# Quarter numbers of the overflow lists from a copy in SBUF instead of four further loads

## What is computed

```python
logits = (xf @ w_router) + b_router                 # 512 x 32
top_val, top_idx = lax.top_k(logits, 4); gates = softmax(top_val)
for e in range(32):                                 # each over the tokens that chose e
    hu  = x_e @ w_gate_up[e] + b_gate_up[e]          # 1024 -> 2048
    act = a * sigmoid(1.702 * a) * (lin + 1)         # a, lin: clamped halves of hu
    y  += gate * (act @ w_down[e] + b_down[e])       # 1024 -> 1024
```

## Time and profile before

| | us |
|---|---|
| median of three runs | 1307.02 |
| the three runs | 1302.45, 1307.02, 1308.0 |
| the profiled execution | 1307.7 |
| its span, first to last instruction | 1305.9 |
| TensorE matmul busy | 1267.0 (97%) |
| VectorE busy | 577.8 (44%) |
| GpSimd busy | 313.9 (24%) |
| ScalarE busy | 177.3 (14%) |
| moved by DMA | 450.85 MB, 345 GB/s over the span |

### The profile page before, as it was taken

The page is one execution under the profiler, slowest core; times in us unless marked ns, Lnnn a source line. Parts: engine busy times, 40 slices in busy tenths (PEclk is TensorE's granted clock), DMA queues, the critical chain, the costliest instruction groups (busy, mean ns, idle before and its releaser), DMA issues.

```text
span 1305.9 us, 32785 instructions
## 1 busy us (share of the span) xinstructions
PE 1267.0 (97%) x13828; PEld 648.3 (50%) x13828; DVE 577.8 (44%) x977; ACT 177.3 (14%) x254; POOL 313.9 (24%) x315
## 2 busy tenths in 40 slices
PE   6999999999999999999999999999999999999996
PEld 6867777763455444444444443333433333433442
DVE  7676655554444344333333333333333333433435
ACT  5143434310000000000000000000000000000002
POOL 2035522001333332222222222222222222222210
PEclk9999999989999999999999999999999999999998
DMA  9222114579999999999999999999999999999984
GB/s 261 67 65 65 65 65 159 229 302 403 414 415 413 401 375 418 416 421 415 414 412 413 415 417 421 417 418 419 422 419 417 418 417 418 418 418 416 418 361 149
DMA packets 95710, 450.85 MB, mean 345 GB/s; under 512 B 12288, under 2 KB 37360, under 8 KB 46528
## 3 DMA queue, kind: packets, MB, share of 16 engines
q1 hardware_dynamic: 83856, 428.37, 80.5%
q0 software_dynamic: 9760, 19.56, 5.7%
q10 hardware_dynamic: 2064, 2.50, 0.5%
HBM read 440.13 MB, written 18.67 MB: 351 GB/s over the span
## 4 chain that ended last, share of the span: by engine, by line
PE 67%; DMA 27%; DVE 3%; issue 1%; ACT 1%; SPq 1%; DVEq 0%; ACTq 0%
PE gu_bank L1707 32%; DMA raw<-in_w_gate_up_dram 26%; PE bank L1721 15%; PE bank L1481 4%; PE bank L1483 4%; PE bank L1482 4%; PE first_gu_bank L1707 2%; PE bank L1558 1%; PE bank L1572 1%; SPq L417 1%; PE bank L1535 1%; PE bank L1683 1%; PE bank L1724 0%; PE bank L1544 0%; PE bank L1492 0%
## 5 line engine op out<-in xcount | busy, mean ns | idle before, releaser
L1707 PE MATMUL gu_bank<-raw,xT 128*32 128x512 f32 x2976 | 328.5, 593 | 8.5 <-DMA raw<-in_w_gate_up_dram 8.5
L1360 DVE TENSOR_TENSOR gate_in<-gu_bank,b_gu 128x768 f32<-128x768 f32 x31 | 29.7, 958 | 540.0 <-PE gu_bank L1707 540.0
L1707 PEld LDWEIGHTS gu_bank<-raw,xT 128*32 128x32 f32 x2976 | 104.3, 110 | 226.7 <-issue 183.0
L613 POOL DMA_INDIRECT x_got<-xn_rows,gather_list x96 | 114.4, 1192 | 329.1 <-DVE xT L1371 295.7
L1721 PE MATMUL bank<-raw_a,aT 128*32 128x256 f32 x2232 | 166.4, 379 | 0.0
L1707 PE MATMUL gu_bank<-raw_c,xT 128*32 128x512 f32 x1488 | 165.7, 592 | 0.0
L1724 PE MATMUL bank<-raw_a,aT 128*32 128x256 f32 x744 | 165.6, 379 | 0.0
L1721 PEld LDWEIGHTS bank<-raw_a,aT 128*32 128x32 f32 x2232 | 101.2, 110 | 67.7 <-issue 17.4
L902 ACT ACTIVATE sig_in<-gate_in 128x768 f32<-128x768 f32 x32 | 27.0, 845 | 634.0 <-DVE gate_in L1364 634.0
L1707 PEld LDWEIGHTS gu_bank<-raw_c,xT 128*32 128x32 f32 x1488 | 53.2, 110 | 106.4 <-issue 96.5
L623 POOL DMA_INDIRECT sum_rows<-y_out,scatter_list x31 | 46.6, 1504 | 186.9 <-ACT y_out L909 94.8
(11 more groups left out here) (267 smaller groups left out, 1620.1 us busy)
## 6 DMA issues: line engine op xcount, KB each, us to landing
raw<-in_w_gate_up_dram SPq DMA_DIRECT2D x128, 1024.0 KB, 27.7
raw_c<-in_w_gate_up_dram SPq DMA_DIRECT2D x62, 1024.0 KB, 26.0
raw_a<-in_w_down_dram SPq DMA_DIRECT2D x62, 1024.0 KB, 27.6
raw_b<-in_w_gate_up_dram SPq DMA_DIRECT2D x32, 1024.0 KB, 26.1
raw_b<-in_w_down_dram SPq DMA_DIRECT2D x32, 1024.0 KB, 26.9
raw_e<-in_w_gate_up_dram SPq DMA_DIRECT2D x31, 1024.0 KB, 27.3
raw_d<-in_w_down_dram SPq DMA_DIRECT2D x31, 1024.0 KB, 26.8
raw<-in_w_in_dram SPq DMA_DIRECT2D x24, 512.0 KB, 6.3
```

The source lines that it names most:

```text
L613: pool.indirect_dma_start(out=x_got[:, r, :], out_offset=None, in_=xn_quarters, in_offset=bass.IndirectOffsetOnAxis(ap=gather_list[:, r:r ...
L1360: dve.tensor_tensor(gate_in[:, :, :], gu[:, :, 0:QUARTER], gate_b, ALU.add)
L1707: ins = pe.matmul(gu[c * GROUP:(c + 1) * GROUP, r, :], x[:, i, r * GROUP:(r + 1) * GROUP], w[:, c], start=first, stop=last)
```

## The change

The loads into list_q go, and with them list_q, quarter_of and its memsets. After the one load into lists_sb, GpSimd makes the quarter numbers from it with twelve tensor_scalars: for each group r of 32 rows and each quarter c it reads the tokens on partitions 32r to 32r+31 of lists_sb (every second word) and writes 4 x token + c to partitions 32c to 32c+31 of rows_q. Each of the twelve waits for the one before.

```diff
-            list_q = lists_only.enter_context(nc.sbuf_tensor("list_q", [P, GROUPS, PLACES - E, 2], U32))
-        quarter_of = sb("quarter_of", [P, 1])
@@ after the memset of x_got
-            pool.wait_ge(x_got_cleared, 1)
-            for c in range(COLS):
-                pool.memset(quarter_of[c * GROUP:(c + 1) * GROUP, :], float(c)).then_inc(quarters_made, 1)
-                pool.wait_ge(quarters_made, c + 1)
@@ def load_overflow():
                 pool.dma_start(lists_sb[0:TILE, 2 * E:2 * PLACES],
                                lists.rearrange("(s j) c -> s (j c)", s=TILE)[:, 2 * E:2 * PLACES])\
                     .then_inc(lists_held, 16)
-                overflow = lists.rearrange("(r t j) w -> t r j w", r=GROUPS, t=GROUP)[:, :, E:PLACES, :]
-                for c in range(COLS):
-                    pool.dma_start(list_q[c * GROUP:(c + 1) * GROUP, :, :, :], overflow).then_inc(lists_held, 16)
-                pool.wait_ge(lists_held, 16 * (1 + COLS))
-                pool.wait_ge(quarters_made, COLS)
-                pool.tensor_scalar(rows_q[:, :, E:PLACES], list_q[:, :, :, 0], float(COLS), quarter_of[:, :],
-                                   ALU.mult, ALU.add).then_inc(rows_q_made, 1)
-                pool.wait_ge(rows_q_made, GROUPS * COLS + 1)
+                pool.wait_ge(lists_held, 16)
+                tokens = lists_sb[:, 2 * E:2 * PLACES].rearrange("s (j two) -> s j two", two=2)[:, :, 0]
+                for r in range(GROUPS):
+                    for c in range(COLS):
+                        pool.tensor_scalar(rows_q[c * GROUP:(c + 1) * GROUP, r, E:PLACES], tokens[r * GROUP:(r + 1) * GROUP, :],
+                                           float(COLS), float(c), ALU.mult, ALU.add).then_inc(rows_q_made, 1)
+                        pool.wait_ge(rows_q_made, GROUPS * COLS + COLS * r + c + 1)
```

More of the change, by code:

```diff
@@ L276, in build @@
         got_turned, x_turned, x_gained = sem("got_turned"), sem("x_turned"), sem("x_gained")
-        quarters_made, rows_q_made = sem("quarters_made"), sem("rows_q_made")
+        rows_q_made = sem("rows_q_made")
         gu_taken, gate_clamped, lin_clamped = sem("gu_taken"), sem("gate_clamped"), sem("lin_clamped")
```

## The result

| | us |
|---|---|
| changed kernel, median of 4 runs | 1315.85 (1315.36 to 1317.77) |
| kernel before, median of 4 runs beside it | 1306.45 |
| ratio | 1.0088, 95% interval 1.0070 to 1.0106 |
| profiled execution of the changed kernel, its span | 1315.36, 1313.6 |

What follows compares the result with a forecast made beforehand. DMA backlog was taken to bound the late jobs. Profiled 1307.7 - 4.4 (list loads) + 0 (GpSimd) + 0 (addresses) = 1303.3 us; as a median 1307.0 - 4.4 = 1302.6 us, 8-in-10 range 1299.0 to 1308.0.

Steps and rivals of the forecast that it cites:

- The reading of what bounds the kernel: From about 400 us DMA is never out of work and has slightly more to do per job than TensorE gives time for.
- landing time as gauge of backlog: Weight load's time from issue to landing shows DMA backlog; climbs 1.06 us a job, TensorE waits at 28.4 us.
- lost time kept to the end: DMA time spent once, at any time after about 400 us, is still there at the end.
- The lists' term: Removing the four list_q loads, in flight around 450 to 464 us, saves 4.4 us; bounds 1.4 to 5.5.
- The share of 4 in 5: Four of five equal list loads were charged by count with 4/5 of the 5.45 us excess: 4.4 us.
- rival (b): Dent split otherwise: lists_sb makes most, 1305.6 us (chance 0.07), or list_q makes all, 1300.5 to 1301.5 us (0.10).
- the first wait for a weight load: Sign: TensorE's first wait on a load comes three to seven jobs later than 751 us.
- GpSimd's part: Twelve tensor_scalars from about 456.5 us take 5 us (4.8 to 9.6); gather for job 7 has cover, so 0 us.
- Moved, addresses: Without quarter_of all behind it, eight of twelve ring slots included, slides 32 bytes: costs 0 to 0.2%, taken as 0.
- rival (c): Weight loads into eight of twelve slots move more slowly after the 32-byte shift: about 1317 us; chance 0.05.
- a climb of landing time other than 1.06 us a job: Sign that the prediction is wrong: the landing time's climb per job changes from 1.06 us, meaning alignment.

Runs made afterwards that it cites:

- e9: Kernel before with four more list loads of 144 KB, each into 32 partitions of a second tensor: 1308.9 us, ratio 1.0026.
- e1: Changed kernel with 32 unused bytes where quarter_of lay, so later addresses are those of the kernel before: 1301.6 us, ratio 0.9969.
- f4: Changed kernel with the 32 bytes put back, the same kernel as e1, in another group of runs: 1302.72 us, ratio 0.9978.
- e3: Kernel before with quarter_of allocated last of the small tensors, so these slide 32 bytes and the overlay stays: 1305.57 us, ratio 0.9999.
- e10: Kernel before with four more list loads of 144 KB, each into 96 partitions: 1308.58 us, ratio 1.0023.
- f2: Changed kernel with 32 unused bytes ahead of x_got alone: x_got on 256, ring slots 224 past: 1310.48 us, ratio 1.0042.
- f3: Changed kernel with the 32 bytes put back and 224 unused bytes ahead of x_got alone: 1302.56 us, ratio 0.9975.
- e4: Changed kernel with the 32 bytes put back and 128 more ahead of raw01 and of the overlay, all twelve slots on 256: 1297.54 us, ratio 0.9934.
- g4: The same kernel as e4 once more, in another group of runs: 1299.12 us, ratio 0.9948.
- g3: Changed kernel with the 32 bytes put back, plus 128 unused bytes ahead of the overlay: 1309.66 us, ratio 1.0038.
- (g): g3 against g1, 128 and 32 unused bytes ahead of the overlay, on the changed kernel with its 32 bytes put back: 1309.66 and 1314.17 us.
- (e): 128 against 32 unused bytes ahead of the overlay (32 is e5), both on the kernel before: ratios 1.0013 and 1.0055.
- f1: Changed kernel once more, ring slots and x_got both 224 past 256: 1316.25 us, ratio 1.0065.
- g1: Changed kernel with the 32 bytes put back, plus 32 unused bytes ahead of the overlay: 1314.17 us, ratio 1.0069.
- e5: Kernel before with 32 unused bytes ahead of the overlay: ratio 1.0055.
- e8: Kernel before with x_got's, gate_in's, y_out's and b_dn's groups 224 bytes further, ring slots left on 256: ratio 0.9998.

## Why the prediction was wrong, step by step

**The reading of what bounds the kernel held.** DMA behind a TensorE that looks 97% busy, landing time as gauge of backlog, lost time kept to the end: e9 and e1 bear it out in both directions, and the 13 us themselves are such time.

**The lists' term was about right: 4.4 forecast, 4.0 and 2.9 measured with addresses kept** (e1, f4), 3.4 in e9. The share of 4 in 5 is not shown. In e1 the gauge loses 5.9 of its jump of 6.5, which is the whole excess and is what rival (b) had for list_q alone; the first wait for a weight load comes at 1028.69 us in e1 and 965.91 in f4, nine and seven jobs after that of the kernel before, where three to seven were forecast (e3, with the slots and loads of before, has it at 844.66, so this sign is coarse). The time at the end says 3 to 4 us. The Trainium skill's rule on ports ("SBUF — State Buffer", "Door 1: The DMA port swizzle"), by which I had estimated 4.8 us, is neither borne out nor excluded: e9 and e10 have 3.4 and 3.0 us, with intervals that overlap.

**GpSimd's part held.** Twelve instructions 5.25 us (forecast 5), no waiting caused.

**The step that failed is "Moved, addresses ... costs 0 to 0.2%, and I take 0".** It costs 13 us, three times the gain: in each job the weights' queue moves 1.5% less, which the sign I had named for it, a climb of landing time other than 1.06 us a job, showed at once (1.25). I had this as rival (c), at 1317 us where 1315.85 was measured. Its kind was right, its place only in part (x_got's gathers pay too, f2 and f3), and its price agrees by luck: the 2.3% between 418 and 428 GB/s is there with all on 256 as well (f4's twelfths have a mean of 417, because of the dip to 341 in the fifth). I gave it 0.05, because the earlier trace rows showed 427 GB/s while slots of raw, 128 past 256, were filled and 428 while others were. Two things were wrong with that reading. It took for granted that the loss goes with the slot that is being filled. The table of twelfths shows that it goes with the time in the job, and both stretches of the earlier trace rows reach into times where even the changed kernel moves 422 to 429. And it took raw01 for a stand-in: in e4 and g4 the queue shows at most 0.2 MB for raw01 at 128 past, while the overlay at 128 past costs 0.7 MB in five jobs (g3). I should have seen that no row could tell: neither a slot of the overlay nor x_got stood off 256 in the trace of before, so the cost was an unknown without an upper bound, and with 250 loads of 1 MB going into those eight slots, half a per cent of a job's time (29 x 30.96 x 0.5% = 4.5 us) decides the sign. A chance of 0.3 or more for (c), and a range up to 1319, was what the rows allowed.

The Trainium skill's rule ("DMA: Bandwidth & Descriptors", "How a descriptor splits into AXI transactions") speaks of what a transaction reads; here the source in HBM stayed and the destination moved, and a start off 256 bytes costs all the same. Its amounts don't fit: worked out from it, as an estimate, 8 KB take 257, 258, 260 and 263 bus beats in place of 256 at 32, 64, 128 and 224 past (260 is 1.6%, where I had written 1.5%), a cost that grows with the distance, and the weights moved are 60.62, 60.62, 60.76 and 60.52 MB against 61.5. Nor does it account for raw01.

## What to carry to other kernels

A removed buffer is two changes: what it did, and where everything behind it in memory goes. Put unused bytes in its place first and measure that, above all where DMA never rests, since 1.5% of the weights' rate is 13 us here; and start the destinations of large loads on 256 bytes. The change with its 32 bytes put back is a gain of 0.2 to 0.3%, with raw01, and all up to the overlay with it, 128 bytes further, 0.5 to 0.7% (e4, g4), the fastest version found.

## What the runs showed of the hardware that was not expected

- The cost of a start off 256 bytes doesn't grow with the distance: 0.7 to 0.95 MB of 61.5 in five jobs for 32, 64, 128 and 224 bytes, with 128 the cheapest by time, 4.5 us (g) and 5.1 us (e) less than 32.
- It depends on the place and the time: at most 0.2 MB for raw01's four slots at 128 past, next to nothing in twelfths 6 to 8 of a job, up to 17 or 18 GB/s of 424 to 429 in the first two. The mechanism is open.
- Chips differ in TensorE's pace at the same granted clock (0.99): 30.96 us a job in e1 to e4, f1 to f4, e9 and e10, the same in g1 to g4 but for single jobs of up to 31.9, and mostly 31.6 in e5 to e8, whose chip took 1313 us for the kernel before; a shift of 128 bytes cost 1.7 us there and about 8 on the chip of g3. Why is open.
